# Opening of a two-layer trunk kernel: one square moved to ScalarE, one subtraction moved off GpSimd, the second pair of scale products moved behind the first columns

## The reference, cut to what matters

```
sh1, sc1, ... = split(silu(c) @ mod_w[0] + mod_b[0], 6)        # c for the latent tokens, c_ctx for the context
h  = rms_norm(x,  norm1_g[0]) * (1 + sc1)  + sh1               # 256 x 1024
hc = rms_norm(cx, norm1_g[0]) * (1 + csc1) + csh1              # 256 x 1024
q, k, v, glu = split(h @ ev_w_in[0], ...)                      # 1024 x 2560, and the same for hc
rms_norm(x, g) = x * rsqrt(mean(x * x) + 1e-6) * g
```

## Time and profile before

| | us |
|---|---|
| median of 3 runs | 1187.4 (1187.0 to 1189.1) |
| the profiled execution | 1187.6 |
| its span | 1185.8 |
| PE busy | 1157.7 (98% of the span) |
| DVE busy | 693.6 (58%) |
| ACT busy | 485.3 (41%) |
| POOL busy | 13.9 (1%) |

### The profile page before, as it was taken

The page is one execution under the profiler, slowest core; times in us unless marked ns, Lnnn a source line. Parts: engine busy times, 40 slices in busy tenths (PEclk is TensorE's granted clock), DMA queues, the critical chain, the costliest instruction groups (busy, mean ns, idle before and its releaser), DMA issues.

```text
span 1185.8 us, 17766 instructions
## 1 busy us (share of the span) xinstructions
PE 1157.7 (98%) x7266; PEld 934.1 (79%) x7266; DVE 693.6 (58%) x1159; ACT 485.3 (41%) x744; POOL 13.9 (1%) x20
## 2 busy tenths in 40 slices
PE   8999999999999999999999999999999999999998
PEld 5777766777588888888887767899565898998997
DVE  5699978853643334423323368887789645554455
ACT  3423336552433232222212242367268636443442
POOL 3000000000000000000000000000000000000000
PEclk9999999999999999999999999999999999999999
DMA  9845473125543222332123664344140157655551
GB/s 346 316 152 177 159 251 122 36 82 203 184 139 104 88 76 84 125 123 84 67 80 116 206 198 142 95 119 143 36 143 2 47 178 239 213 177 179 193 167 65
DMA packets 118893, 167.73 MB, mean 141 GB/s; under 512 B 4797, under 2 KB 102695, under 8 KB 114599
## 3 DMA queue, kind: packets, MB, share of 16 engines
q1 hardware_dynamic: 118390, 166.23, 42.1%
q10 hardware_dynamic: 433, 0.51, 0.2%
HBM read 164.37 MB, written 1.05 MB: 139 GB/s over the span
## 4 chain that ended last, share of the span: by engine, by line
PE 85%; DVE 10%; ACT 2%; DMA 2%; issue 1%; SPq 0%; DVEq 0%; ACTq 0%; POOL 0%
PE acc L2153 20%; PE acc L2154 20%; PE acc L2155 20%; PE pmod L2073 2%; PE acc L2232 2%; PE acc L2233 1%; PE acc L2234 1%; PE p L2518 1%; PE p L2519 1%; PE p L2517 1%; DMA first_mod<-in_mod_w 1%; PE p L2006 1%; DVE Y L1429 1%; DVE sm L1511 1%; PE p L2395 1%
## 5 line engine op out<-in xcount | busy, mean ns | idle before, releaser
L646 DVE TENSOR_TENSOR w_lo<-raw,w_hi 128x1024 fp32r<-128x1024 f32 x222 | 249.0, 1163 | 234.8 <-ACT w_hi L636 234.5
L636 ACT ACTIVATE w_hi<-raw 128x1024 fp32r<-128x1024 f32 (+1 forms) x224 | 212.8, 998 | 408.7 <-PE acc L2155 358.2
L2153 PE MATMUL acc<-Hhi,w_hi 128*128 128x512 f32 (+1 forms) x960 | 326.3, 340 | 1.6 <-DVE w_lo L646 1.6
L2155 PE MATMUL acc<-Hhi,w_lo 128*128 128x512 f32 (+1 forms) x960 | 324.3, 338 | 0.0
L2154 PE MATMUL acc<-Hlo,w_hi 128*128 128x512 f32 (+1 forms) x960 | 324.2, 338 | 0.0
L2153 PEld LDWEIGHTS acc<-Hhi,w_hi 128*128 128x128 f32 x960 | 182.1, 190 | 25.7 <-issue 3.9
L2155 PEld LDWEIGHTS acc<-Hhi,w_lo 128*128 128x128 f32 x960 | 182.1, 190 | 19.6
L2154 PEld LDWEIGHTS acc<-Hlo,w_hi 128*128 128x128 f32 x960 | 182.2, 190 | 19.2
L2153 PE MATMUL acc<-hid_hi,w_hi 128*128 128x512 f32 x248 | 97.9, 395 | 0.1
L2154 PE MATMUL acc<-hid_lo,w_hi 128*128 128x512 f32 x248 | 96.6, 390 | 0.0
L2155 PE MATMUL acc<-hid_hi,w_lo 128*128 128x512 f32 x248 | 96.6, 389 | 0.0
(11 more groups left out here) (392 smaller groups left out, 1602.8 us busy)
## 6 DMA issues: line engine op xcount, KB each, us to landing
raw<-in_mod_w SPq DMA_DIRECT2D x44, 1024.0 KB, 5.3
raw<-in_ffn_w_in SPq DMA_DIRECT2D x44, 1024.0 KB, 5.1
raw<-in_od_w_in SPq DMA_DIRECT2D x15, 1024.0 KB, 5.4
raw<-in_ffn_w_out SPq DMA_DIRECT2D x12, 768.0 KB, 4.5
raw<-in_ev_w_in SPq DMA_DIRECT2D x8, 1024.0 KB, 7.5
raw<-in_od_w_out SPq DMA_DIRECT2D x8, 1024.0 KB, 5.9
raw<-in_ffn_w_out SPq DMA_DIRECT2D x8, 1024.0 KB, 5.0
raw<-in_ev_w_out SPq DMA_DIRECT2D x8, 768.0 KB, 6.3
```

Source lines behind the costliest of these rows:

```text
L636: nc.scalar.activation(w_hi[:, w % 2, c0:c1], raw[:, r % RAW_SLOTS, c0:c1], ACT.Copy)\
L646: nc.vector.tensor_tensor(w_lo[:, w % 2, c0:c1], raw[:, r % RAW_SLOTS, c0:c1], w_hi[:, w % 2, c0:c1].bitcast(F32), ALU.subtract).then_inc( ...
L2153: mm(outs[m], hi[:, j, cols], xh, start=(first and j == 0), stop=False)
L2155: ins = mm(outs[m], lo[:, j, cols], xh, start=False, stop=(last and j == kts - 1))
```

## The change

It has three parts.

1. The square of tile 6 goes from DVE to ACT, behind those of 5 and 7 in tile order (5, 6, 7).
2. GpSimd only rounds the first half of block 0. The subtraction becomes `first_lo(0, 0)` on DVE, behind `square0(4)`.
3. `mod_unit(2)` and `(3)` go from ahead of `first_two` to a place inside it, behind the wait for tile 2 of `Hlo` and ahead of the columns of j = 2. `scales_T(1)` goes from ahead of block 0's j = 3 to ahead of block 1's j = 1. On DVE `scales_copy(1)` goes from behind `low0(1)` to behind `low0(3)`, right ahead of `first_gains(1)`. The semaphores are dealt out anew: units 0 and 1 wait for one transfer each, units 2 and 3 both for the last two.

```
 first_scales:  .then_inc(s(f"scales_loaded{max(i - 1, 0)}"), 16)   ->   s(f"scales_loaded{min(i, 2)}")
 mod_unit:      pe.wait_ge(s(f"scales_loaded{max(m - 1, 0)}"), 32 if m < 2 else 16)
            ->  pe.wait_ge(s(f"scales_loaded{min(m, 2)}"), 16 if m < 2 else 32)

-SQ_DVE, SQ_POOL, SQ_ACT = (0, 2, 4, 6), (1, 3), (5, 7)
+SQ_DVE, SQ_POOL, SQ_ACT = (0, 2, 4), (1, 3), (5, 6, 7)

 # GpSimd
 nc.gpsimd.tensor_copy(w_hi[:, 0, 0:1024], raw[:, 0, 0:1024]).then_inc(hi_split, 1)
-pool.wait_ge(hi_split, 1)
-nc.gpsimd.tensor_tensor(w_lo[:, 0, 0:1024], raw[:, 0, 0:1024], w_hi[:, 0, 0:1024].bitcast(F32), ALU.subtract)
-    .then_inc(lo_split, 1)

 # ACT
 for f in SQ_ACT:
-    act.wait_ge(s("xT_act"), f // 2 + 1)
+    act.wait_ge(s("xT_act") if f % 2 else s("xT_dve"), f // 2 + 1)

 # DVE
 square0(4)
-square0(6)
+first_lo(0, 0)
...
 low0(1)
-scales_copy(1)
 gained0(3)
-dve.wait_ge(lo_split, 1)
 first_lo(1, 0)
 low0(3)
+scales_copy(1)
 first_gains(1)
 first_lo(0, 1)
 first_lo(1, 1)

 # PE
 spread_roots(0, T)
-mod_unit(2)
-mod_unit(3)
...
 for j in range(4):
     pe.wait_ge(s("h_lo_dve") if j < 2 else s("h_lo"), j + 1)
-    if j == 3:
-        scales_T(1)
+    if j == 2:
+        mod_unit(2)
+        mod_unit(3)
     for m in range(2):
         column(0, j, m)
 pe.wait_ge(lo_split, FIRST[1, 0])
 for j in range(4):
+    if j == 1:
+        scales_T(1)
     for m in range(2):
         ins = column(1, j, m)
```

More of the change, by code:

```diff
@@ L480, in first_scales @@
                 sp.dma_start(first_mod[i][:, :].rearrange("p (k n) -> p k n", k=4),
-                             tiles(a["mod_w"][0, rows_:rows_ + 4 * P, cols_:cols_ + 4 * P])).then_inc(s(f"scales_loaded{max(i - 1, 0)}"), 16)
+                             tiles(a["mod_w"][0, rows_:rows_ + 4 * P, cols_:cols_ + 4 * P])).then_inc(s(f"scales_loaded{min(i, 2)}"), 16)
             def first_block(r, part, loaded):
@@ L701, in _ @@
             nc.gpsimd.tensor_copy(w_hi[:, 0, 0:1024], raw[:, 0, 0:1024]).then_inc(hi_split, 1)
-            pool.wait_ge(hi_split, 1)
-            nc.gpsimd.tensor_tensor(w_lo[:, 0, 0:1024], raw[:, 0, 0:1024], w_hi[:, 0, 0:1024].bitcast(F32), ALU.subtract)\
-                .then_inc(lo_split, 1)
             for f in range(KD):
@@ L2030, in mod_unit @@
                 if m < 4:
-                    pe.wait_ge(s(f"scales_loaded{max(m - 1, 0)}"), 32 if m < 2 else 16)
+                    pe.wait_ge(s(f"scales_loaded{min(m, 2)}"), 16 if m < 2 else 32)
                     if m == 0:
```

## The result

The changed kernel takes 1194.8 us (median of 6, 1193.67 to 1195.84), the kernel before 1187.52 (median of 6). The ratio is 1.006 with a 95% interval of 1.0047 to 1.0073: 7.3 us slower, or 0.6%. The prediction said slower by 3.2 us, with a range up to 1192.8. The sign was right, the size was not.

What follows compares the result with a forecast made beforehand. The prediction took PE's stream as the bound, in balance with the DMA arc to unit 7 at 41.2 us. Arc 1.9 later plus clock fall 1.3 made 1187.4 + 3.2 = 1190.6 us, range 1187.0 to 1192.8.

Steps and rivals of the forecast that it cites:

- The start: Opening up to the first column: unit 0 directly behind sum 3, root near 18.9, first column 24.3 instead of 26.67.
- The arc: Chain from scales_T(1) over DVE's gains and two subtractions and SP's transfer to unit 7: 1.9 us later.
- The turn: scales_T(1) on PE: starts at 33.15 instead of 31.25 without the clock, 1.9 us later.
- the last transfer: Last shift weights, issued by SP after the two subtractions: landing at 43.15 instead of 41.24, releasing unit 7.
- The clock: TensorE's clock expected to fall again, over the first columns after PE's thin stretch from 19.9 to 24.3: 1.3 us lost.
- The first fall: Clock fall over the first columns, ahead of scales_T(1): 1.3 us taken, between 0.5 and 1.75.
- The second fall: Rival: PE idles 2.5 to 3 us ahead of units 6 and 7, then half clock: 1.5 us more, 1192.1; 15%.
- No fall: Rival: no clock fall over the columns, PE being denser between 16 and 20: +1.9, 1189.3 us; 27%.
- PE decides: Rival: last shift transfers land by 40.5, so PE's arrival at unit 4 counts: 0.8 us faster, 1186.6; 10%.
- The start is not earlier: Rival: tile 4's square stays slow, first column 0.7 to 1.2 later: 1190.3 without a fall, 1191.6 with one; 5%.

Runs made afterwards that it cites:

- e8: The changed kernel with unread matmuls on PE, 5 behind spread_roots, 2 ahead of unit 6, 5 ahead of unit 7; 1190.67 us.
- e1: The changed kernel with first_lo(0, 1) and (1, 1) on DVE ahead of scales_copy(1) and first_gains(1); 1188.87 us.
- e5: The changed kernel with 5 unread matmuls on PE behind spread_roots only; 1193.15 us.
- e3: The kernel before with part 3 of the change alone, including its new semaphores; 1196.33 us.
- e9: The changed kernel, but SP waits for unit 7 before it issues the next weight block and what is behind it; 1195.08 us.
- e10: The changed kernel with first_lo(0, 1) and (1, 1) ahead of first_gains(1) on DVE, and 5 unread matmuls on PE behind spread_roots; 1186.60 us.
- e7: The kernel before with first_lo(0, 1) and (1, 1) ahead of first_gains(1) on DVE; 1187.19 us.
- e2: The kernel before with parts 1 and 2 of the change alone; 1187.64 us.

## Why the prediction was wrong

**The start: right.** The square of tile 4 fell from 2.25 to 0.68 us (0.87 reckoned), unit 0 ran at 16.73, the root was at 19.22 (18.9 reckoned; this execution runs 0.2 behind from the start), the first column at 24.52 (24.3).

**The arc: right in mechanism, short by 1.1.** The turn is 2.1 us later without the clock (e8), where 1.9 was reckoned. DVE's idle time, the two subtractions, SP's wait and unit 7 released by DMA came as described, and e1 confirms it by undoing it. But I carried the last transfer over at its 6.80 us, and it took 7.70 to 7.94 in every kernel that issues it late. That is a row of before used for a moment in which the queue's state was another.

**The clock: this is the step that failed.** The first fall was sized well: I took 1.3 us, and the timelines give 1.4 (e5's median 1.65 to 1.8). The second fall, behind units 6 and 7, I made a rival with 15% and 1.5 us. It is in the profiles of the changed kernel, e3, e5 and e9, and it is worth 2.5 us (by the medians of e5 and e8; in the changed kernel's profile 0.86 on unit 7 itself and 1.7 on the columns up to 51 us). The sum put it at nothing, and this is the largest part of the 4.1 us between forecast and result. Its low clock lasted 6.8 us in the changed kernel, and I had taken the 3.5 us of the one fall in the earlier trace rows as the length of any. The inconsistency was in my own text: I worked out that PE would stand idle for 2.5 to 3 us there (it was 3.5), and had taken 2.4 us of nothing plus a thin stretch before it as likely to make the clock fall in the first place. The rows show the same thing twice: 1.25 us of work in 4.4 and in 4.7 us, with 2.5 and 2.6 us of nothing at the end.

| term, us | reckoned | measured | from |
|---|---|---|---|
| turn later, full clock | 1.9 | 2.1 | e8 against before |
| this execution late from its start | 0 | 0.2 | first column at 24.52, in e8 at 24.32 |
| first fall | 1.3 | 1.4 | first column to turn, 10.39 against 9.03 in e8 |
| last transfer longer | 0 | 0.9 | 7.70 - 6.80 |
| second fall | 0 (rival: 1.5) | 2.5 | 0.86 + 1.7 |
| sum | 3.2 | 7.1 | 7.04 on DVE at 61.6 and 68.6 |

**The rivals.** "No fall" is refuted by the changed kernel's own windows, and e5 shows its price. What was said for it came true, the fall of before at 18.5 did not come; but a new one came in the hole. "PE decides" did not happen, unit 7 waited 2.6 us for its transfer; it becomes true only once the subtractions are moved, and then PE's stream gives about what was said for it (-0.8 reckoned, -1.1 in e10, with the doubt told of there). "The start is not earlier" did not happen; e3 shows what it would have cost, 1.3 us. The Trainium skill, "TensorE: Matmul & The Clock Gate", section "What's actually happening", says that the slow clock is the default and that activity is what releases it. The traces agree: both falls came in holes of PE (0.51), and with fillers in the holes the same stretches have 1.00 (e8).

## What to carry to other kernels

Work that is moved out of an engine's idle time costs twice: once in the stream to which it goes, and once in the hole it leaves, if the engine is TensorE and the hole lowers its clock. Before a wait is moved later, look at what is queued behind the waiting instruction on its own engine; here two subtractions that needed nothing from it held up two transfers, and exchanging the lines gave 6 of 7.3 us back. And when the reckoning yields an idle stretch, ask of it what was asked of every other one.

## What the runs showed of the hardware

- In the changed kernel the clock fell in standstills of PE of 2.5 and 2.6 us, before PE had work again, in stretches in which PE was busy 1.25 us of 4.4 and 1.25 of 4.7. It stayed low until 27.4 in one place and for 6.8 us in the other. In e5's profile the second fall came at 45.0, half a microsecond after unit 7 had begun behind 2.85 us of idle time, and lasted 3.4 us.
- Whether a hole lowers the clock differs between executions of nearly the same code. The one at 309 us of the kernel before (PE busy 1.4 us of 2) was followed by a fall in the profiles of the changed kernel, e1 and e9, and not in the ten others. In the opening, the fall at 18.5 of the earlier trace rows came behind 1.23 us of idle time ahead of unit 0; in e7's profile unit 0 had 1.64 us of idle time ahead of it, and the clock stayed at 1.00.
- DVE's square of 128 x 512 took 0.68 us with GpSimd idle, 0.87 where it began while GpSimd's rounding copy ran, and 2.25 while GpSimd's subtraction ran, where it ended 0.55 us after that did. With the subtraction taken from GpSimd and the rest of the opening as before (e2) it took 0.68.
- A pair of 1024 KB transfers was seen complete 8.0 us after its first issue in the kernel before, 8.8 to 9.0 where its queue had moved no packet for 2.3 to 3.5 us (changed kernel, e8, e9), and 8.5 and 8.7 where the queue was busy (e1, e10). The first of the pair took no longer in the late cases (5.1 to 5.4 us). e9 excludes the transfers issued behind the pair as the reason; the reason stays open.
